# A two-block transformer kernel on one Trainium2 core: tokens loaded feature-major in place of sixteen transposes, token-major rows loaded behind weight blob 2

## The chip, the core and the metric

One core of a Trainium2 chip. Five engines run side by side, each with an instruction stream of its own, tied together by semaphores: TensorE (PE, matmuls out of SBUF into PSUM), VectorE (DVE), ScalarE (ACT), GpSimd (POOL) and SyncE (SP), which issues DMAs. ACT issues some DMAs too. A DMA moves data between HBM and SBUF and raises its semaphore by 16 when it has landed. The metric is device microseconds for one execution.

## The reference

A token block x of 256 tokens by 1024 features (float32) goes through two transformer layers of different make. What matters here is the very beginning, the first layer's norm and its input projection:

```python
def rmsnorm(x, gain):
    xf = x.astype(jnp.float32)
    y = xf * lax.rsqrt(jnp.mean(xf * xf, axis=-1, keepdims=True) + NORM_EPS)
    return (y * gain.astype(jnp.float32)).astype(x.dtype)
...
    proj = jnp.einsum('bsd,dn->bsn', xn, w_in)
    q_a, k_a, v_a, q_r, k_r, v_r, g_r, gate_a, gate_r = jnp.split(proj, IN_OFFSETS, axis=-1)
...
    h = x
    for l in range(DEPTH):
        h = h + mixer_block(rmsnorm(h, norm_mix_gain[l]), w_in[l], b_gates[l], attn_sinks[l],
                            ret_gn_gain[l], w_att_up[l], w_ret_up[l], w_out[l], att_rope, ret_rope)
        h = h + squared_relu_mlp(rmsnorm(h, norm_mlp_gain[l]), w_ff1[l], w_ff2[l])
```

Behind it come attention with a window, retention, gates, a feed-forward layer, and then a whole second block with its own weights. The change touches nothing of these.

## The kernel before, in words

**Weights.** All weight matrices are one stream of blobs of 128 partitions by 2048 float32 (1 MB each), numbered n = 0, 1, 2, ... SP loads blob n into `raw` (four buffers in the first layer). Every matmul is made of three products of float32r numbers: a number is split in a high part and a rest. ACT writes `whi` = high part of `raw` (function `hi`, L701), DVE writes `wlo` = `raw` - `whi` (function `lo`, L1621), and PE computes high x high (L477), high x rest (the line that the trace shows as L478 or L479) and rest x high for each piece (helper `product`, called by `multiply_tokens`). SP loads blob n + 4 into the buffer of blob n once `lo(n)` is done.

**Tokens.** `h` [128, 2, 1024] holds the 256 tokens token-major: partition = token in a tile of 128, two tiles t. A matmul that contracts over features needs them feature-major: `xT_h` and `xT_l` (high part and rest of gain times x), eight chunks k of 128 features by 256 tokens. The factor 1/rms of each token is applied after the matmul, by `stat`, when results leave PSUM.

**The start.** Before the change PE turns `h` into feature-major form: 16 transposes of 128x128 (`pieces(0, ...)`, L1185), two to a piece, eight pieces, listed in `XT_ORDER[0]` and placed in PSUM banks by `XT_PLACE[0]`. ACT scales each piece by the gain and writes `xT_h` (L717); DVE writes `xT_l` from the same PSUM piece (`to_pieces`, L1655). Blobs 0 and 1 are loaded and split in the parts of the table `FIRST` (blob, first chunk, last chunk + 1): five parts. PE multiplies part by part with pieces of transposes between them. Blob 0 feeds chunks 0 to 3 and blob 1 chunks 4 to 7; each chunk is 6 matmuls of 512 columns, so the two are 48. Blob 2 is 48 matmuls of 256 columns over all eight chunks, and every later blob of the projection is 24 matmuls of 512 columns. Before the first piece PE runs matmuls on zeros (`keep_warm`, L1207).

**The norm.** ACT squares the lower half of `h` with a running sum (L707), DVE the upper half (`square_upper`, L1630), DVE adds the shares (L1641) and POOL makes 1/rms (L1124). ACT waits for that before it takes the first results out of PSUM (L779).

**What sets the order.** Each engine runs its program in the order in which it is written. On DVE the two `square_upper` stand in front of `lo(2)`; on ACT `hi(2)` stands in front of the two squares and `hi(3)` behind them. On SP the DMAs are issued one after another on one queue; ACT issues the load of the first quarter of `h`. The load of `h` is in four quarters of the features, on the semaphores `x_in[0..3]`.

Of the kernel before, what the change touches and what calls it, by code (L numbers as in the profile page):

```python
# [80 lines left out]
for _name, _width in (("sinks", A_HEADS * 2), ("sinks_2", S_HEADS), ("lambdas", 4 * DH)):  # L81
# [3 lines left out]

XT_ORDER = (((0, 0), (1, 0), (0, 2), (1, 2), (0, 4), (1, 4), (0, 6), (1, 6)),
# [3 lines left out]
XT_PLACE = ((2, 3, 4, 5, 6, 7, 2, 3), (2, 3, 4, 6, 2, 3, 5, 7), (0, 1, 4, 6, 0, 1, 5, 7), (2, 3, 4, 5, 6, 7, 4, 5))  # L90

FIRST = ((0, 0, 1), (0, 1, 2), (0, 2, 4), (1, 0, 2), (1, 2, 4))

# [59 lines left out]

def build(nc, w, x, meta, consts, turns, rows, grow, out):

    with ExitStack() as ctx:
        def sem(name):
            return ctx.enter_context(nc.semaphore(name))
# [478 lines left out]
        def _(sp):  # L637
# [7 lines left out]

            def load_tokens(q):

                sp.dma_start(h[:, :, q * TOK:(q + 1) * TOK], x[:, :, q * TOK:(q + 1) * TOK]).then_inc(x_in[q], 16)

# [6 lines left out]
            load_first(1)  # L656
            load_tokens(1)
            load_first(2)
            load_tokens(2)
            load_first(3)  # L660
            load_tokens(3)
            load_first(4)
            load(2, w[2], None)
            load(3, w[3], None)
            sp.dma_start(cst[:, EARLY:NCONST], consts[:, EARLY:NCONST]).then_inc(const_in, 16)
# [27 lines left out]
        def _(act):  # L693
# [17 lines left out]
            def to_pieces(r, gain, pieces):  # L711

                for i in pieces:
                    act.wait_ge(xt_ps, 8 * r + i + 1)
                    t, k0 = XT_ORDER[r][i]
                    for k in range(2):
                        act.activation((xT_h if r < 2 else x2_h)[:, k0 + k, t * P:(t + 1) * P], piece(r, i, k), ACT.Copy,  # L717
                                       scale=cl(gain, k0 + k)).then_inc(xt_hi, 1)
# [30 lines left out]

            act.dma_start(h[:, :, 0:TOK], x[:, :, 0:TOK]).then_inc(x_in[0], 16)  # L750

            act.wait_ge(init_ok, 1)
            act.activation(lam[:], kaT[:, 0, 0:4], ACT.Copy)
            def first_part(i):
# [4 lines left out]
                               ACT.Copy).then_inc(split_hi if end == 4 else first_hi, 1)  # L759

            act.wait_ge(early_in, 16)
            to_pieces(0, "norm_mix", (0, 1))
            first_part(1)
            first_part(2)
            to_pieces(0, "norm_mix", (2, 3))
            to_pieces(0, "norm_mix", (4, 5))
            first_part(3)
            first_part(4)
            to_pieces(0, "norm_mix", (6, 7))
            hi(2)  # L770
            square(0)
            square(1)
# [392 lines left out]
        def _(pe):  # L1165
            ident = c("ident")

            def pieces(r, which):

                for i in which:  # L1170
                    t, k0 = XT_ORDER[r][i]
                    if r == 0:
                        pe.wait_ge(x_in[k0 // 2], 16)
                        if i >= 6:
                            pe.wait_ge(xt_lo, 2 * (i - 5))
                    elif r < 3:
                        pe.wait_ge(h_ok, 4 * (r - 1) + 2 * (k0 // 4) + t + 1)
# [44 lines left out]
            pe.wait_ge(early_in, 16)  # L1222
            pieces(0, (0, 1))
            keep_warm(2, 1, warm)
            for i, (n, k, end) in enumerate(FIRST):
                pe.wait_ge(split_lo if end == 4 else first_lo, first_made(i))
                multiply_tokens(pe, n, 4 * n, 4, BANK, 0, n == 0, n == 1, xT_h, xT_l, 0, ks=range(k, end))
                if i < 3:
                    pieces(0, (2 * i + 2, 2 * i + 3))
            for n in range(2, MIX1):  # L1230
# [377 lines left out]
        def _(dve):  # L1608
# [239 lines left out]
            def first_part(i):  # L1848
# [3 lines left out]
                if i:  # L1852
                    dve.wait_ge(split_hi if end == 4 else first_hi, first_made(i) - (end < 4))
                dve.tensor_tensor(wlo[n][:, a:b], raw[n][:, a:b], whi[n][:, a:b],  # L1854
                                  ALU.subtract).then_inc(split_lo if end == 4 else first_lo, 1)

            dve.wait_ge(early_in, 16)
            dve.wait_ge(first_in[0], 16)
            link(dve, "dve", dve.tensor_copy(whi[0][:, 0:BANK], raw[0][:, 0:BANK]))
            first_part(0)  # L1860
            to_pieces(0, "norm_mix", (0, 1))
            first_part(1)
            first_part(2)
            to_pieces(0, "norm_mix", (2, 3))
            to_pieces(0, "norm_mix", (4, 5))
            first_part(3)
            first_part(4)
            to_pieces(0, "norm_mix", (6, 7))
            dve.wait_ge(x_in[2], 16)
            dve.wait_ge(x_in[3], 16)  # L1870
            square_upper(0)
# [183 lines left out]
            dve.wait_ge(row_in, 32)  # L2055
            dve.wait_ge(xt_ps, 24)
            dve.wait_ge(rstd_ok, norms[0])
# [381 lines left out]
```

## Time and profile before

| what | value |
|---|---|
| median of 3 runs | 885.03 us (882.45, 885.03, 885.08) |
| the profiled execution's own time | 883.24 us |
| its span, first to last instruction | 881.6 us |
| PE busy | 871.6 us (99%) |
| DVE busy | 622.4 us (71%) |
| ACT busy | 459.4 us (52%) |
| DMA | 154.64 MB, mean 175 GB/s |

The span is the time from the first instruction to the last; 1.6 us lie around it. PE is busy nearly throughout, with its clock granted in full on the page, and DVE and ACT prepare the blobs ahead of it. The bandwidth is 345 and 401 GB/s in the first two slices of 22 us and about 200 GB/s after them.

### The profile page before, as it was taken

To read this page: it belongs to the slowest core of one execution; us is meant where nothing else is said; L and a number is where in the kernel's file an instruction comes from. 1 tells how busy PE (TensorE), PEld (TensorE's weight loads), DVE (VectorE), ACT (ScalarE), POOL (GpSimd) and SP (SyncE) were. 2 spreads that over 40 slices of the span, in tenths; PEclk is the share of its full clock that TensorE was granted. 3 is DMA by queue.
4 is the path that set the end of the run, shared out by engine and by line. 5 is a ranking of instruction groups with operands and counts; after the bars stand their busy time and mean duration, and the time that the engine had idled before them with its cause. 6 is when DMAs were issued, how large, how long until landed. Compare 5 with 4: busy or idle time off the path is not lost.

```text
span 881.6 us, 12940 instructions
## 1 busy us (share of the span) xinstructions
PE 871.6 (99%) x4790; PEld 730.9 (83%) x4790; DVE 622.4 (71%) x994; ACT 459.4 (52%) x742; POOL 45.2 (5%) x81
## 2 busy tenths in 40 slices
PE   8999999999999999999999999999999999999997
PEld 5887788888888888889998777777888888888886
DVE  6867677665876666668855778887766876666665
ACT  6546534334744444444546666677643654444443
POOL 0100010000200000002000000122300100000000
PEclk9999999999999999999999999999999999999999
DMA  9954344553565555343662223423274365555441
GB/s 345 401 206 180 128 159 143 191 191 143 205 237 193 188 192 190 145 167 122 215 254 98 101 114 115 148 97 144 96 262 174 109 233 184 187 195 187 186 143 48
DMA packets 24733, 154.64 MB, mean 175 GB/s; under 512 B 2912, under 2 KB 4192, under 8 KB 7280
## 3 DMA queue, kind: packets, MB, share of 16 engines
q1 hardware_dynamic: 22224, 146.61, 46.1%
q10 hardware_dynamic: 2464, 7.42, 2.3%
q8 instruction: 29, 0.48, 0.2%
q14 instruction: 16, 0.13, 0.0%
HBM read 151.58 MB, written 1.05 MB: 173 GB/s over the span
## 4 chain that ended last, share of the span: by engine, by line
PE 94%; DVE 3%; ACT 1%; DMA 1%; issue 0%; DVEq 0%; SPq 0%; ACTq 0%
PE ps L477 21%; PE ps L479 20%; PE ps L478 20%; PE ps L597 15%; PE ps L599 8%; PE ps L1510 2%; PE ps L1436 1%; PE ps L1460 1%; PE ps L1185 1%; DMA raw<-weights 1%; DVE sc L1820 1%; PE ps L614 1%; PE ps L1455 1%; DVE wlo L1621 0%; ACT sc L960 0%; PE ps L1450 0%
## 5 line engine op out<-in xcount | busy, mean ns | idle before, releaser
L1621 DVE TENSOR_TENSOR wlo<-raw,whi 128x2048 fp32r<-128x2048 f32 x134 | 306.7, 2290 | 148.5 <-ACT whi L701 148.1
L701 ACT ACTIVATE whi<-raw 128x2048 fp32r<-128x2048 f32 x134 | 256.4, 1916 | 182.5 <-PE ps L479 114.5
L477 PE MATMUL ps<-whi,xT 128*128 128x512 f32 (+1 forms) x224 | 88.0, 393 | 0.5 <-DVE xT L1655 0.5
L479 PE MATMUL ps<-whi,xT 128*128 128x512 f32 (+1 forms) x224 | 85.8, 383 | 0.0
L478 PE MATMUL ps<-wlo,xT 128*128 128x512 f32 (+1 forms) x224 | 85.6, 382 | 0.0
L597 PE MATMUL ps<-x_all,whi 128*128 128x512 f32 x336 | 84.0, 392 | 0.0
L597 PEld LDWEIGHTS ps<-x_all,whi 128*128 128x128 f32 x336 | 61.0, 189 | 11.3
L477 PE MATMUL ps<-whi,x_all 128*128 128x512 f32 x160 | 65.8, 411 | 0.4 <-ACT qbT L967 0.2
L597 PE MATMUL ps<-xT,whi 128*128 128x512 f32 x256 | 64.5, 392 | 0.0
L479 PE MATMUL ps<-whi,x_all 128*128 128x512 f32 x160 | 62.6, 391 | 0.0
L478 PE MATMUL ps<-wlo,x_all 128*128 128x512 f32 x160 | 62.4, 390 | 0.0
L597 PEld LDWEIGHTS ps<-xT,whi 128*128 128x128 f32 x256 | 46.3, 189 | 8.5
L477 PE MATMUL ps<-whi,fT_h 128*128 128x512 f32 x128 | 50.3, 393 | 0.0
L477 PEld LDWEIGHTS ps<-whi,xT 128*128 128x128 f32 x224 | 42.1, 188 | 9.7 <-DVE wlo L1854 1.3
L478 PE MATMUL ps<-wlo,fT_h 128*128 128x512 f32 x128 | 49.9, 390 | 0.0
L479 PE MATMUL ps<-whi,fT_l 128*128 128x512 f32 x128 | 49.8, 389 | 0.0
L479 PEld LDWEIGHTS ps<-whi,xT 128*128 128x128 f32 x224 | 42.1, 188 | 8.5
L599 PEld LDWEIGHTS ps<-x_all,wlo 128*128 128x128 f32 x336 | 45.8, 190 | 3.3
L478 PEld LDWEIGHTS ps<-wlo,xT 128*128 128x128 f32 x224 | 42.2, 188 | 7.5
L960 ACT ACTIVATE sc<-sc,usoft 128x272 f32<-128x272 f32 x64 | 32.7, 512 | 28.1 <-DVE usoft L1829 14.1
L599 PE MATMUL ps<-x_all,wlo 128*128 128x256 f32 x336 | 46.8, 282 | 0.0
L477 PE MATMUL ps<-x_all,whi 128*128 128x272 f32 x160 | 46.7, 292 | 0.0
(323 smaller groups left out, 1628.5 us busy)
## 6 DMA issues: line engine op xcount, KB each, us to landing
raw<-weights SPq DMA_DIRECT2D x134, 1024.0 KB, 4.8
raw<-weights SPq DMA_DIRECT2D x3, 512.0 KB, 7.3
cst<-consts SPq DMA_DIRECT2D x1, 1499.0 KB, 14.0
kswap<-kraw SPq DMA_DIRECT2D x20, 68.0 KB, 2.0
gate_a<-gain_rows ACTq DMA_DIRECT2D x2, 512.0 KB, 7.1
gate_r<-gain_rows ACTq DMA_DIRECT2D x2, 512.0 KB, 5.2
gate_s<-gain_rows ACTq DMA_DIRECT2D x2, 512.0 KB, 7.8
gate_d<-gain_rows ACTq DMA_DIRECT2D x2, 512.0 KB, 4.3
```

The lines of the kernel that those rows point to most:

```text
L477: pe.matmul(o, lh, rh, start=first, stop=False)
L478: pe.matmul(o, lh, rl, start=False, stop=False)
L479: return pe.matmul(o, ll, rh, start=False, stop=last)
L597: pe.matmul(ps[:, bank0 + j, :], vh[:, k, j * P:(j + 1) * P], x[:, :, k, :], start=k == 0, stop=False)
L599: m = pe.matmul(ps[:, bank0 + j, 0:TOK], vl[:, k, j * P:(j + 1) * P], x[:, 0, k, :], start=False, stop=k == KC - 1)
L614: pe.matmul(o, vh[:, k, j * P:(j + 1) * P], x[:, :, k, t * P:(t + 1) * P], start=k == 0, stop=False)
L701: act.activation(whi[s][:], raw[s][:], ACT.Copy).then_inc(split_hi, 1)
L960: ins = act.activation(scores(U, u), scores(U, u), ACT.Exp, bias=st[:, 2, u:u + 1], accum_out=st[:, 4, u:u + 1])
L1185: m = pe.transpose(piece(r, i, k), h[:, t, (k0 + k) * P:(k0 + k + 1) * P], ident)
L1436: pe.transpose(ps[:, 6, (2 * u + kt) * P:(2 * u + kt + 1) * P], scores_of_tile(U, u, kt), ident)
L1510: m = pe.matmul(ps[:, 4 + u, 0:KEYS], qT[half, cc, t * P:(t + 1) * P], kT, start=True, stop=True)
L1621: dve.tensor_tensor(wlo[s][:], raw[s][:], whi[s][:], ALU.subtract).then_inc(split_lo, 1)
```

## The change

The host passes x a second time, as `x_features`: 128 partitions by 8 chunks by 256 tokens, feature-major. SP and ACT load it in four quarters into a new tile `xF` (which lies where `gr` comes later), on `x_in[0..3]`. ACT and DVE make `xT_h` and `xT_l` straight from `xF`, a chunk of 128x256 at a time (`features_hi`, `features_lo`), where they read 128x128 pieces of PSUM before. PE does no transposes for this round; the other rounds of transposes stay. The token-major `h` is still needed by the norm and the residual: SP loads it whole, 1 MB in one DMA on a new semaphore `tok_in`, behind blob 2 and ahead of blob 3. ACT waits for `tok_in` between `hi(2)` and the squares; DVE waits for it in front of `square_upper`, which still stands ahead of `lo(2)`. Blob 0 is loaded and split in four parts where it was three.

```diff
-XT_ORDER = (((0, 0), (1, 0), (0, 2), (1, 2), (0, 4), (1, 4), (0, 6), (1, 6)),
+XT_ORDER = ((),
...
-FIRST = ((0, 0, 1), (0, 1, 2), (0, 2, 4), (1, 0, 2), (1, 2, 4))
+FIRST = ((0, 0, 1), (0, 1, 2), (0, 2, 3), (0, 3, 4), (1, 0, 2), (1, 2, 4))
...
+        xF = at("xF", [P, KC, TOK], F32, gr_at)
...
-            def load_tokens(q):
-
-                sp.dma_start(h[:, :, q * TOK:(q + 1) * TOK], x[:, :, q * TOK:(q + 1) * TOK]).then_inc(x_in[q], 16)
+            def load_features(q):
+
+                sp.dma_start(xF[:, 2 * q:2 * q + 2, :], x_features[:, 2 * q:2 * q + 2, :]).then_inc(x_in[q], 16)
...
             load_first(0)
             load_first(1)
-            load_tokens(1)
+            load_features(1)
             load_first(2)
-            load_tokens(2)
             load_first(3)
-            load_tokens(3)
+            load_features(2)
             load_first(4)
+            load_features(3)
+            load_first(5)
             load(2, w[2], None)
+            sp.dma_start(h[:], x).then_inc(tok_in, 16)
             load(3, w[3], None)
...
-            act.dma_start(h[:, :, 0:TOK], x[:, :, 0:TOK]).then_inc(x_in[0], 16)
+            act.dma_start(xF[:, 0:2, :], x_features[:, 0:2, :]).then_inc(x_in[0], 16)
...
+            def features_hi(q):
+
+                act.wait_ge(x_in[q], 16)
+                for k in (2 * q, 2 * q + 1):
+                    act.activation(xT_h[:, k, :], xF[:, k, :], ACT.Copy, scale=cl("norm_mix", k)).then_inc(xt_hi, 2)
+
             act.wait_ge(early_in, 16)
-            to_pieces(0, "norm_mix", (0, 1))
+            features_hi(0)
             first_part(1)
+            features_hi(1)
             first_part(2)
-            to_pieces(0, "norm_mix", (2, 3))
-            to_pieces(0, "norm_mix", (4, 5))
             first_part(3)
+            features_hi(2)
             first_part(4)
-            to_pieces(0, "norm_mix", (6, 7))
+            features_hi(3)
+            first_part(5)
             hi(2)
+            act.wait_ge(tok_in, 16)
             square(0)
             square(1)
...
             pe.wait_ge(early_in, 16)
-            pieces(0, (0, 1))
             keep_warm(2, 1, warm)
             for i, (n, k, end) in enumerate(FIRST):
                 pe.wait_ge(split_lo if end == 4 else first_lo, first_made(i))
-                multiply_tokens(pe, n, 4 * n, 4, BANK, 0, n == 0, n == 1, xT_h, xT_l, 0, ks=range(k, end))
-                if i < 3:
-                    pieces(0, (2 * i + 2, 2 * i + 3))
+                pe.wait_ge(xt_lo, 2 * (4 * n + end))
+                multiply_tokens(pe, n, 4 * n, 4, BANK, 0, n == 0, n == 1, xT_h, xT_l, ks=range(k, end))
...
+            def features_lo(*ks):
+
+                for k in ks:
+                    dve.wait_ge(xt_hi, 2 * (k + 1))
+                    dve.scalar_tensor_tensor(out=xT_l[:, k, :], in0=xF[:, k, :], scalar=cl("norm_mix", k),
+                                             in1=xT_h[:, k, :], op0=ALU.mult, op1=ALU.subtract).then_inc(xt_lo, 2)
+
             dve.wait_ge(early_in, 16)
+            features_lo(0)
             dve.wait_ge(first_in[0], 16)
             link(dve, "dve", dve.tensor_copy(whi[0][:, 0:BANK], raw[0][:, 0:BANK]))
             first_part(0)
-            to_pieces(0, "norm_mix", (0, 1))
+            features_lo(1)
             first_part(1)
+            features_lo(2, 3)
             first_part(2)
-            to_pieces(0, "norm_mix", (2, 3))
-            to_pieces(0, "norm_mix", (4, 5))
             first_part(3)
+            features_lo(4, 5)
             first_part(4)
-            to_pieces(0, "norm_mix", (6, 7))
-            dve.wait_ge(x_in[2], 16)
-            dve.wait_ge(x_in[3], 16)
+            features_lo(6, 7)
+            first_part(5)
+            dve.wait_ge(tok_in, 16)
             square_upper(0)
             square_upper(1)
             lo(2)
```

How the instructions stand in a row. SP, the queue of DMA issues from its second instruction on, before. `raw_49`, `raw_52`, `raw_55` and `raw_58` are the buffers of blobs 0, 1, 2 and 3:

```order
L644 DMA cst<-consts 128x250
L653 DMA raw_49<-weights 128x512 x2
L648 DMA h<-x_tiles 128x2x256
L653 DMA raw_49<-weights 128x1024
L648 DMA h<-x_tiles 128x2x256
L653 DMA raw_52<-weights 128x1024
L648 DMA h<-x_tiles 128x2x256
L653 DMA raw_52<-weights 128x1024
L642 DMA raw_55<-weights 128x2048
L642 DMA raw_58<-weights 128x2048
```

SP, the same place after:

```order
L646 DMA cst<-consts 128x250
L655 DMA raw_49<-weights 128x512 x2
L650 DMA xF<-x_features 128x512
L655 DMA raw_49<-weights 128x512 x2
L650 DMA xF<-x_features 128x512
L655 DMA raw_52<-weights 128x1024
L650 DMA xF<-x_features 128x512
L655 DMA raw_52<-weights 128x1024
L644 DMA raw_55<-weights 128x2048
L667 DMA h<-x_tiles 128x2048
L644 DMA raw_58<-weights 128x2048
```

The quarters of `xF` stand where quarters of `h` stood, and the whole `h` takes the place that blob 3 had.

DVE from its third instruction on, the splits of blobs 0 to 2, before. `wlo_51`, `wlo_54` and `wlo_57` are the rests of blobs 0, 1 and 2; the two ISA lines with `xn` are `square_upper`:

```order
L1859 CAST whi_50<-raw_49 128x512
L1854 TENSOR_TENSOR wlo_51<-raw_49,whi_50 128x512
L1655 SCALAR_TENSOR_TENSOR xT<-ps,cst,xT 128x128 x4
L1854 TENSOR_TENSOR wlo_51<-raw_49,whi_50 128x512
L1854 TENSOR_TENSOR wlo_51<-raw_49,whi_50 128x1024
L1655 SCALAR_TENSOR_TENSOR xT<-ps,cst,xT 128x128 x8
L1854 TENSOR_TENSOR wlo_54<-raw_52,whi_53 128x1024 x2
L1655 SCALAR_TENSOR_TENSOR xT<-ps,cst,xT 128x128 x4
L1630 ISA xn,stat<-h 128x512
...
L1621 TENSOR_TENSOR wlo_57<-raw_55,whi_56 128x2048
```

DVE, the same place after:

```order
L1867 SCALAR_TENSOR_TENSOR xT<-xF,cst,xT 128x256
L1873 CAST whi_50<-raw_49 128x512
L1860 TENSOR_TENSOR wlo_51<-raw_49,whi_50 128x512
L1867 SCALAR_TENSOR_TENSOR xT<-xF,cst,xT 128x256
L1860 TENSOR_TENSOR wlo_51<-raw_49,whi_50 128x512
L1867 SCALAR_TENSOR_TENSOR xT<-xF,cst,xT 128x256 x2
L1860 TENSOR_TENSOR wlo_51<-raw_49,whi_50 128x512 x2
L1867 SCALAR_TENSOR_TENSOR xT<-xF,cst,xT 128x256 x2
L1860 TENSOR_TENSOR wlo_54<-raw_52,whi_53 128x1024
...
L1636 ISA xn,stat<-h 128x512
...
L1627 TENSOR_TENSOR wlo_57<-raw_55,whi_56 128x2048
```

The first rest of x stands ahead of blob 0's first part; one chunk of it, where four pieces were, stands between the first two parts; the squares of `h` still stand ahead of the split of blob 2.

## Rows read from the trace of the kernel before

**Rows 1.** PE's waits over the whole span; columns: engine, tile, line, releaser, us, times, longest.

```profile
PE ps L1207 <- DVE kaT L1847: 1.4, 1, 1.4
PE ps L1185 <- DMA h<-x_tiles: 1.2, 1, 1.2
PE ps L477 <- DVE xT L1655: 0.5, 1, 0.5
```

**Rows 2.** Timeline, 0 to 10 us: start, us, engine, line, operation, tiles, count [idle before].

```profile
5.96 0.63 PE L1185 MATMUL ps<-cst,h 128*128 128x128 f32 x4 [1.21 <-DMA h<-x_tiles]
6.47 1.14 ACT L717 ACTIVATE xT<-ps,cst 128x128 fp32r<-128x128 f32 x4 [3.56 <-PE ps L1185]
6.76 0.43 DVE L1859 CAST whi<-raw 128x512 fp32r<-128x512 f32 x1 [5.37 <-DMA raw<-weights]
7.22 0.69 DVE L1854 TENSOR_TENSOR wlo<-raw,whi 128x512 fp32r<-128x512 f32 x1
7.83 1.12 DVE L1655 SCALAR_TENSOR_TENSOR xT<-ps,cst,xT 128x128 fp32r<-128x128 f32 x4
8.84 0.47 PE L477 MATMUL ps<-whi,xT 128*128 128x512 f32 x1 [0.53 <-DVE xT L1655]
```

**Rows 3.** Timeline, PE: behind the last transposes, first of blob 2, first of blob 3.

```profile
15.95 0.50 PE L477 MATMUL ps<-whi,xT 128*128 128x512 f32 x1
...
21.54 0.39 PE L477 MATMUL ps<-whi,xT 128*128 128x256 f32 x1
...
27.38 0.40 PE L477 MATMUL ps<-whi,xT 128*128 128x512 f32 x1
```

**Rows 4.** All groups of instructions by form: line, forms, count, busy us, mean ns.

```profile
L1934 DVE SCALAR_TENSOR_TENSOR retT_l<-ps,cst,retT_h 128x256 fp32r<-128x256 f32 x8 | 3.5, 478 | 5.5 <-ACT retT_h L838 5.5
L838 ACT ACTIVATE retT_h<-ps,cst 128x256 fp32r<-128x256 f32 x8 | 3.3, 466 | 5.9 <-PE ps L1331 5.9
```

**Rows 5.** Timeline, ACT and DVE, 16 to 23 us: splits of blobs 2 and 3, squares.

```profile
16.97 1.93 ACT L701 ACTIVATE whi<-raw 128x2048 fp32r<-128x2048 f32 x1
...
17.98 0.68 DVE L1630 CUSTOM_DVE_ANT_0 xn<-h 128x512 f32<-128x512 f32 x1
...
19.20 2.29 DVE L1621 TENSOR_TENSOR wlo<-raw,whi 128x2048 fp32r<-128x2048 f32 x1
```

**Rows 6.** DMA issues and landings: tiles, queue, count, KB, us from issue to landing.

```profile
h<-x_tiles ACTq DMA_DIRECT2D x1, 256.0 KB, 5.1
...
raw<-weights SPq DMA_DIRECT2D x1, 1024.0 KB, 9.6
...
raw<-weights SPq DMA_DIRECT2D x1, 1024.0 KB, 11.6
...
raw<-weights SPq DMA_DIRECT2D x1, 1024.0 KB, 12.9
```

**Rows 7.** Timeline, SP's queue, the issues of blobs 2, 3 and, from 11.94, 4 and later.

```profile
6.24 0.91 SPq L642 DMA_DIRECT2D raw<-weights  x2
```

**Rows 8.** Busy time of three stretches: us, engines, PEclk, DMA share, GB/s (last).

```profile
3.00:5.50 2.50, 1.75 (x3) 0.34 (x1) 0.00 (x0) 0.00 (x0) 0.00 (x0) 1.00 0.74 168
5.50:8.00 2.50, 2.04 (x8) 1.07 (x8) 1.20 (x3) 1.53 (x5) 0.00 (x0) 1.00 1.03 383
8.00:18.00 10.00, 9.47 (x46) 7.44 (x46) 8.28 (x21) 7.41 (x17) 0.00 (x0) 1.00 1.04 421
```

**Rows 9.** Timeline, PE's weight loads for the matmuls on zeros, one to each matmul.

```profile
3.32 0.34 PEld L1207 LDWEIGHTS ps<-kaT 128*128 128x128 f32 x1 [0.52 <-issue]
...
7.29 0.19 PEld L1207 LDWEIGHTS ps<-kaT 128*128 128x128 f32 x1 [0.24 <-issue]
```

**Rows 10.** Timeline, 24 to 35 us: splits of blob 4 and PE's first matmul on it.

```profile
25.91 1.92 ACT L701 ACTIVATE whi<-raw 128x2048 fp32r<-128x2048 f32 x1
...
28.15 2.29 DVE L1621 TENSOR_TENSOR wlo<-raw,whi 128x2048 fp32r<-128x2048 f32 x1
...
33.87 0.48 PE L477 MATMUL ps<-whi,xT 128*128 128x512 f32 x1
```

More of the change, by code:

```diff
@@ L89 @@
             ((0, 0), (0, 2), (0, 4), (0, 6), (1, 0), (1, 2), (1, 4), (1, 6)))
-XT_PLACE = ((2, 3, 4, 5, 6, 7, 2, 3), (2, 3, 4, 6, 2, 3, 5, 7), (0, 1, 4, 6, 0, 1, 5, 7), (2, 3, 4, 5, 6, 7, 4, 5))
-FIRST = ((0, 0, 1), (0, 1, 2), (0, 2, 4), (1, 0, 2), (1, 2, 4))
+XT_PLACE = ((), (2, 3, 4, 6, 2, 3, 5, 7), (0, 1, 4, 6, 0, 1, 5, 7), (2, 3, 4, 5, 6, 7, 4, 5))
+FIRST = ((0, 0, 1), (0, 1, 2), (0, 2, 3), (0, 3, 4), (1, 0, 2), (1, 2, 4))
 def first_made(i):
@@ L151, in fills, with build @@
     return (N1 - 1) // 4 + 1 + (n - N1) // 3
-def build(nc, w, x, meta, consts, turns, rows, grow, out):
+def build(nc, w, x, x_features, meta, consts, turns, rows, grow, out):
     with ExitStack() as ctx:
@@ L323, in build @@
         x_in = [sem(f"x_in{i}") for i in range(4)]
+        tok_in = sem("tok_in")
         early_in = sem("early_in")
@@ L713, in to_pieces @@
                 for i in pieces:
-                    act.wait_ge(xt_ps, 8 * r + i + 1)
+                    act.wait_ge(xt_ps, 8 * (r - 1) + i + 1)
                     t, k0 = XT_ORDER[r][i]
@@ L1171, in pieces @@
                     t, k0 = XT_ORDER[r][i]
[L1172 to L1176, printed above, removed]
+                    if r < 3:
                         pe.wait_ge(h_ok, 4 * (r - 1) + 2 * (k0 // 4) + t + 1)
@@ L2055, in _ @@
             dve.wait_ge(row_in, 32)
-            dve.wait_ge(xt_ps, 24)
+            dve.wait_ge(xt_ps, 16)
             dve.wait_ge(rstd_ok, norms[0])
@@ L2407 @@
     x = i["x"][0].reshape(NT, P, D).transpose(1, 0, 2)
+    x_features = i["x"][0].T.reshape(KC, P, TOK).transpose(1, 0, 2)
     consts = constants()
@@ L2425 @@
         "x_tiles": x,
+        "x_features": x_features,
         "meta": i["meta_tokens_2"],
```

## The prediction, written before the changed kernel was run

> **What bounds the kernel now.** I read the waits of PE first [rows 1]. Over 881.6 us PE has three waits of 0.5 us or more, all in the first 9 us; what the view has beside them is 0.4 and 0.2. Everything after 8.84 us is one unbroken run of matmuls, so a microsecond that PE starts earlier, or is kept waiting once, should move the end by one microsecond. Then I read the timeline of the start [rows 2]. The chain to the first real matmul is: quarter 0 of `h` lands (5.96), PE transposes it, ACT makes the high parts (6.47), DVE meanwhile splits the first part of blob 0 (6.76 to 7.91) and only then makes the rests (7.83), and PE begins at 8.84. Last come the reads ahead of blob 2 [rows 3, 5]: PE starts blob 2 at 21.54 without a pause, and DVE ends the split of blob 2 at 19.20 + 2.29 = 21.49. The two meet within 0.05 us. That is the row on which my forecast hangs: PE cannot gain anything at this point unless `lo(2)` is earlier too.
>
> **Part 1: the transposes go.** Between 15.95 and 21.54 PE does 24 matmuls in 5.59 us, 0.233 us each [rows 3]. All 48 of blobs 0 and 1 are 11.18 us. From 8.84 to 21.54 they took 12.70, so the three groups of transposes between them cost 1.52 us in all. This goes away. The fourth group runs ahead of the first matmul and leaves the chain with it.
>
> **Part 2: the first matmul.** Quarter 0 now feeds ACT directly. It was issued at about 0.74 and landed 5.1 us later, 5.84 [rows 6]. No row has an activation of 128x256 from SBUF; from PSUM it takes 466 ns, and the matching DVE operation 478 ns [rows 4]. I take these, with 0.3 to 0.6 as bounds: the high part of chunk 0 at 6.35, its rest at 6.85. The first part of blob 0 was there at 6.76 [rows 2]; cast and rest take 0.43 + 0.69, so with handovers of about 0.03 each PE starts at 8.05. That is 0.8 us earlier (bounds 0.5 and 1.0). The Trainium skill, "VectorE: DVE Perf Modes", section "The TRN2 errata — SBUF-src ops pay a fixed extra latency per instruction", gives SBUF sources a smaller fixed cost than PSUM on VectorE (58 cycles against 120) and a larger one on ScalarE (224 against 172). An estimate by its figures puts the start 0.1 us earlier than mine and leaves the end of the forecast as it is. No run here shows it yet.
>
> **Part 3: supply of the eight chunks.** DVE's work on x shrinks from 16 operations to 8, blob 0 in four parts adds one. With landings as before, walking DVE's order in steps of 0.40 for a rest and 0.69 or 1.2 for a part gives: chunk 1 ready 9.1 (PE wants it 9.5), chunk 2 10.7 (10.9), chunk 3 11.3 (12.3), chunks 4 and 5 about 13.9 (13.7), chunks 6 and 7 about 15.9 (16.5). At most 0.3 us of stall. So PE would be through with blob 1 at 8.05 + 11.18 + about 0.2 = 19.4, some 2.1 us before 21.54. This is the whole prize of the change, and the trace of before has no other place for more.
>
> **Part 4: blob 2, where it is lost.** DVE waits for `tok_in` before the squares, and `lo(2)` is behind them. ACT has `hi(2)` ahead of its own wait, so that is not in the way. When does `h` land? Bytes ahead of and including it on the queue: constants 0.13 MB, blobs 0 and 1 2.10, features 1.05, blob 2 1.05, `h` 1.05: 5.37 MB. Before, the same sum up to and including blob 3 was 0.13 + 2.10 + 1.05 (tokens) + 1.05 + 1.05: 5.37 MB. `h` takes the place that blob 3 had. Blob 2 was issued at 6.24 and blob 3 about 0.48 later, at 6.72 [rows 7]; they landed 9.6 and 11.6 us after that [rows 6], at 15.8 and 18.3. The 2.5 us between them for 1.05 MB are 420 GB/s, and the ten microseconds up to 18.00 run at 421 GB/s with a DMA share of 1.04 [rows 8], so the DMA engines are full and nothing hides there. The quarters now have runs of 2 KB where they had 1 KB, which can only help; from 3.00 to 5.50 the rate is 168 GB/s at a share of 0.74, and from 5.50 it is 383 [rows 8]. If the low rate came from short runs, those 2.5 us could shrink by up to 1.4; if from starting up, by nothing, since DMA engines were partly idle then. I take 0.1: `h` lands at 18.2.
> From the start of the squares to the end of `lo(2)` DVE took 21.49 - 17.98 = 3.51 us [rows 5]. So `lo(2)` ends at 18.2 + 0.05 + 3.51 = 21.76 and PE starts blob 2 at about 21.8, where it was 21.54. PE waits some 2.4 us at this point, a wait that is new. The sum: -0.8 (start), -1.5 (transposes), +0.2 (chunk stalls), +2.4 (wait for blob 2) = **+0.3 us**. All of what is gained in parts 1 and 2 is given back in one wait. Bounds: -1.1 if the DMA start shrinks by all of 1.4, +0.6 if `h` is late by 0.3.
>
> **Part 5: behind blob 2.** The queue now carries 1.05 MB more ahead of everything later, 2.5 us at 421 GB/s. Blob 3 lands near 20.7; ACT and DVE have its rest at about 25, PE wants it at 27.6 (21.8 + 27.38 - 21.54). Blob 4, issued at 11.94, landed 12.9 later [rows 6], 24.8; now 27.3. Its high part began at 25.91 and begins at 27.3, its rest began at 28.15 and begins at about 29.2, ready 31.5 [rows 10]; PE wants it at 33.87 + 0.3. That leaves 2.6 us. The cover is this lead of DVE over PE; gone, each microsecond costs one. ACT waits behind `tok_in` with `hi(3)`, which waits for its own later load anyway. The split of `h` into one DMA, the changed counts of semaphores and the place of `xF` cost nothing: no engine is late at them.
>
> **The rivals.**
> *A, part of the gain stays (2 in 10).* The slow start of the DMAs was due to 1 KB runs, so `h` and blob 2 come up to 1.4 us earlier. `lo(2)` then ends near 20.4 and blob 2 starts near 20.5: up to -1.1. A little more would need DVE not to wait for `h` before `lo(2)`: blob 2 landed at 15.8, `hi(2)` takes 1.93 and `lo(2)` 2.29 [rows 5], so 20.1 and -1.4 would be the limit of an order with `lo(2)` first. The transfer rate above speaks against a large part of it: the engines were not full between 3.00 and 5.50.
> *B, slower: the new wait costs clock (1 in 10).* Matmuls on zeros ran one in 0.34 + 0.52 = 0.86 us at 3.32 and in 0.19 + 0.24 = 0.43 us at 7.29 [rows 9]: 1.2 and 2.4 GHz. The slow work went from 1.4 [rows 1] to 5.96 - 1.21 = 4.75 [rows 2], some 3.3 us, and behind the idle 1.21 us the engine was fast. No gap of 2.4 us stands in this trace once PE is fast. If such a gap takes the clock down and it needs 3.3 to 4.5 us of work to come back, that work takes twice its time: 1.7 to 2.2 us more, +2.0 to +2.5 in all. The 0.5 us ahead of 8.84 did not do it; the granted clock of the whole stretch up to 18.00 is 1.00 [rows 8]. For 2.4 us I have no row, so the case keeps a chance.
> *C, other (under 1 in 10).* Blob 4 or 5 comes more than 2.6 us later than I have it and PE waits a second time (+1 to +2), or DVE's order stalls PE in blob 0 by more than 0.3, which the wait at blob 2 would swallow.
>
> **How the numbers follow.** Forecast 65%, A 18%, B 10%, C 7%. Against the profiled execution: span 881.6 + 0.3 = 881.9, time 883.24 + 0.3 = 883.5. The median shown is 885.03, which is 1.8 above that execution, and the lowest run is 882.45; the spread of the four times, 2.6 us, is larger than any term of mine. On the median the sum is 885.3, on the middle of the four times (884.1) it is 884.4. I take 884.6. The range takes in A (884.1 - 1.1, less what the spread adds) and most of B: 882.2 to 886.8. A measurement of this kernel can tell about 0.3%, 2.65 us. The largest gain that any case holds is 1.1, so faster by that much needs luck with the spread: 5%. Slower needs B or C in full plus some spread: 6%. The rest, 89%, is no change.
>
> **What would show it.** Right: no PE idle time for transposes, first matmul near 8.05, one wait of PE near 19.4 to 21.8 released by `wlo` of blob 2, DVE idle from about 16 to 18.2 for the DMA of `h`, and PE unbroken after. Part 2 is wrong if the first matmul is not within 0.3 us of 8.05; part 3 if PE waits more than 0.5 us inside blobs 0 and 1; part 4 if `h` lands before 17.5 or DVE is not idle ahead of the squares; part 5 if PE waits at blob 3, 4 or 5. If the matmuls behind the wait have twice their spacing, B holds.

## The result, and the profile after

| | before | changed |
|---|---|---|
| median | 883.62 us (882.45 to 885.08, 12 runs) | 886.07 us (884.80 to 887.08, 12 runs) |
| profiled execution: time, span | 883.24, 881.6 | 887.08, 885.0 |
| first matmul on blob 0 | 8.84 us | 7.42 us |
| first matmul on blob 2 | 21.54 us | 23.59 us |

The ratio of changed to before is 1.0022, 95% interval 1.0014 to 1.0030. The changed kernel is some 2 us slower. That is below the 0.3% that I had named as what can be told, but twelve runs tell it from nothing, and I had forecast no change. One run of E9 below took 1447.29 us at a mean granted clock of 0.558 and stands outside every median and ratio here.

The first view is what PE waited for in the changed kernel, over the whole span (columns as in [rows 1]):

```profile
PE ps L479 <- DVE wlo L1627: 2.4, 1, 2.4
PE ps L479 <- DVE wlo L1860: 1.7, 2, 1.4
PE ps L1215 <- DVE kaT L1853: 1.4, 1, 1.4
PE ps L616 <- DVE x_all L1661: 0.4, 1, 0.4
```

L1627 is `lo`, L1860 the split of a part of blobs 0 and 1; in the changed kernel L479 is the product high x high that was L477. The wait for transposes is gone, and so is the one for `xT` in [rows 1]. Two new ones are there: 2.4 us for the rest of blob 2, as forecast, and 1.7 us inside blobs 0 and 1, where I had at most 0.3.

The timeline of the changed kernel, its main steps, in order of time (columns as in [rows 2]):

```profile
4.93 0.91 ACT L769 ACTIVATE xT<-xF,cst 128x256 fp32r<-128x256 f32 x2 [2.26 <-DMA xF<-x_features]
5.58 0.48 DVE L1867 SCALAR_TENSOR_TENSOR xT<-xF,cst,xT 128x256 fp32r<-128x256 f32 x1 [4.19 <-ACT xT L769]
...
7.42 0.84 PE L479 MATMUL ps<-whi,xT 128*128 128x512 f32 x1
...
11.02 0.63 ACT L762 ACTIVATE whi<-raw 128x512 fp32r<-128x512 f32 x1 [2.21 <-DMA raw<-weights]
...
12.43 0.50 PE L479 MATMUL ps<-whi,xT 128*128 128x512 f32 x1 [0.29 <-DVE wlo L1860]
...
15.46 0.50 PE L479 MATMUL ps<-whi,xT 128*128 128x512 f32 x1 [1.38 <-DVE wlo L1860]
...
17.53 1.92 ACT L705 ACTIVATE whi<-raw 128x2048 fp32r<-128x2048 f32 x1 [1.43 <-DMA raw<-weights]
...
20.02 0.69 DVE L1636 CUSTOM_DVE_ANT_0 xn<-h 128x512 f32<-128x512 f32 x1 [2.67 <-DMA h<-x_tiles]
...
21.25 2.29 DVE L1627 TENSOR_TENSOR wlo<-raw,whi 128x2048 fp32r<-128x2048 f32 x1
...
23.59 0.38 PE L479 MATMUL ps<-whi,xT 128*128 128x256 f32 x1 [2.40 <-DVE wlo L1627]
...
36.39 1.03 PE L1222 MATMUL ps<-cst,tok 128*128 128x128 f32 x8
```

The last line is the first transposes behind blob 3. In the kernel before they stand here:

```profile
32.86 1.03 PE L1214 MATMUL ps<-cst,tok 128*128 128x128 f32 x8
```

These answer [rows 2], [rows 3] and [rows 5]. Features are there at 4.93, a microsecond earlier than the quarter of `h` was. Then ACT waits 2.21 us at 11.02 for the fourth part of blob 0, and 1.43 at 17.53 for blob 2. DVE has been idle 2.67 us when `h` lands at 20.02; I had 18.2. From there to PE's first matmul on blob 2 the chain is what was forecast: 3.57 us.

Busy time by stretch of the changed kernel (columns as in [rows 8]; PEclk is third from the end):

```profile
6.00:8.00 2.00, 2.00 (x4) 0.74 (x3) 1.97 (x5) 1.26 (x3) 0.00 (x0) 1.00 1.07 339
8.00:10.00 2.00, 2.00 (x11) 1.62 (x10) 1.53 (x4) 0.81 (x2) 0.00 (x0) 1.00 0.94 245
10.00:12.00 2.00, 2.00 (x10) 1.45 (x8) 0.31 (x1) 0.74 (x2) 0.00 (x0) 1.00 1.04 412
24.00:26.00 2.00, 2.00 (x14) 2.00 (x14) 1.55 (x1) 1.49 (x3) 0.83 (x2) 0.65 1.03 427
26.00:28.00 2.00, 2.00 (x11) 2.00 (x11) 1.90 (x8) 0.19 (x1) 0.00 (x0) 0.50 1.02 426
```

Two things stand here that the sum of the forecast did not have. From 8 to 10 us the DMAs move 245 GB/s with engines that are 94% busy, where the kernel before moved 410 in the same two microseconds. And after the wait for blob 2 the granted clock is 0.50: 1.2 GHz instead of 2.4. Rival B happened.

**Where 3.4 us come from.** From the start of blob 0 to that of blob 2 the kernel before needs 12.70 us, the changed one 23.59 - 7.42 = 16.17. By starts of matmuls: first matmul earlier -1.42; transposes between the matmuls gone -1.52; the first matmuls still slow (7.42 took 0.84, though the granted clock of that stretch reads 1.00) about +0.5; stalls inside blobs 0 and 1 +2.0; wait at blob 2 +2.5. Sum +2.05. From the first matmul on blob 2 to the transposes behind blob 3 it takes 36.39 - 23.59 = 12.80 us, where it was 32.86 - 21.54 = 11.32: +1.48 for half clock. Together 3.5, of 3.4 in the spans. It can be told more shortly: `h` landed 1.8 us later than forecast (20.02 against 18.2), and the chain behind it sets the start of blob 2; so the earlier first matmul and the stalls inside blobs 0 and 1 change only how long PE waits there. Forecast 0.3, late landing 1.8 and half clock 1.5 make 3.6, of 3.4 in the spans. Around the span there is a little more as well: time minus span is 1.58 to 1.71 in every run of the kernel before and 1.78 to 2.11 in the changed one (E1 and E16 included).

### The profile page after: what moved, and what is told of

Read it like the earlier page. It is cut to its first block, busy times and chain, and to the rows that moved or that the text cites. A ratio compares the mean times of both kernels' runs of the same rounds, so it can differ in the third digit from the quotient of the medians.

```text
span 885.0 us, 12903 instructions
## 1 busy us (share of the span) xinstructions
PE 872.8 (99%) x4774; PEld 731.2 (83%) x4774; DVE 621.5 (70%) x987; ACT 459.4 (52%) x735; POOL 43.1 (5%) x81
## 3 DMA queue, kind: packets, MB, share of 16 engines
q10 hardware_dynamic: 2336, 7.42, 2.5%
## 4 chain that ended last, share of the span: by engine, by line
PE 93%; DVE 3%; DMA 1%; SPq 1%; ACT 1%; issue 0%; DVEq 0%; ACTq 0%
PE ps L479 20%; PE ps L481 19%; PE ps L480 19%; PE ps L599 15%; PE ps L601 8%; PE ps L1516 2%; DMA h<-x_tiles 1%; PE ps L1442 1%; PE ps L1466 1%; DVE wlo L1627 1%; PE ps L1193 1%; DVE sc L1826 1%; PE ps L616 1%; PE ps L1461 0%; ACT sc L972 0%
## 5 line engine op out<-in xcount | busy, mean ns | idle before, releaser
L1627 DVE TENSOR_TENSOR wlo<-raw,whi 128x2048 fp32r<-128x2048 f32 x134 | 306.6, 2290 | 151.5 <-ACT whi L705 151.2
L479 PE MATMUL ps<-whi,xT 128*128 128x512 f32 (+1 forms) x224 | 89.0, 397 | 4.1 <-DVE wlo L1627 2.4
L599 PEld LDWEIGHTS ps<-x_all,whi 128*128 128x128 f32 x336 | 61.0, 189 | 11.3
L479 PE MATMUL ps<-whi,x_all 128*128 128x512 f32 x160 | 65.8, 411 | 0.4 <-ACT qsT L979 0.2
L479 PEld LDWEIGHTS ps<-whi,xT 128*128 128x128 f32 x224 | 43.0, 192 | 13.8 <-DVE wlo L1860 3.0
L479 PE MATMUL ps<-whi,fT_h 128*128 128x512 f32 x128 | 50.3, 393 | 0.0
L479 PE MATMUL ps<-x_all,whi 128*128 128x272 f32 x160 | 46.7, 292 | 0.0
```

Source lines behind the costliest of these rows:

```text
L479: pe.matmul(o, lh, rh, start=first, stop=False)
L599: pe.matmul(ps[:, bank0 + j, :], vh[:, k, j * P:(j + 1) * P], x[:, :, k, :], start=k == 0, stop=False)
L1627: dve.tensor_tensor(wlo[s][:], raw[s][:], whi[s][:], ALU.subtract).then_inc(split_lo, 1)
```

## Experiments

All kernels below come from one of the two kernels by the edit shown. Ratios are to the kernel before, with 95% interval. "Lands" is the time of the waiting instruction behind the DMA.

**E1: the same kernel again**, and once more as E16.

> The changed kernel once more, unedited. Theory (the late landing of h belongs to the kernel): first matmul of blob 0 near 7.4 us, rate of the DMAs from 6.5 to 9.5 us again well under 383 GB/s, h lands near 20.0, blob 2 starts near 23.6 and the matmuls behind it run at half clock for some 3.5 us; ratio to before 1.002 to 1.004. Rival (the one profiled execution was an unlucky one): h lands near 18.2, blob 2 starts near 21.8, no half clock.

> The changed kernel, a third profile. Theory: features and four parts make the DMAs slow between 6 and 10 us (rates 245 to 340 GB/s from 8 to 10 us), h lands between 18.6 and 20.0, blob 2 starts between 22.2 and 23.6, PE waits 2.4 us for it; whether half clock follows differs from execution to execution (it did in one of two). Rival: the second profile (h at 18.6) was the rule and 20.0 the exception, or the other way round.

E1: 884.70 us (10 runs), ratio 1.0016 (1.0004 to 1.0027). E1's timeline:

```profile
18.63 0.69 DVE L1636 CUSTOM_DVE_ANT_0 xn<-h 128x512 f32<-128x512 f32 x1 [2.65 <-DMA h<-x_tiles]
...
22.20 0.39 PE L479 MATMUL ps<-whi,xT 128*128 128x256 f32 x1 [2.37 <-DVE wlo L1627]
```

and E16's:

```profile
19.49 0.69 DVE L1636 CUSTOM_DVE_ANT_0 xn<-h 128x512 f32<-128x512 f32 x1 [2.65 <-DMA h<-x_tiles]
...
23.06 0.39 PE L479 MATMUL ps<-whi,xT 128*128 128x256 f32 x1 [2.37 <-DVE wlo L1627]
```

The landing of `h` moves between 18.6 and 20.0 from execution to execution, with rates of 335, 288 and 245 GB/s from 8 to 10 us; the wait at blob 2 is 2.4 us each time. The spans are 882.2, 883.0 and 885.0. E1 and E16 keep the full clock behind the wait, the first profile does not. So the slow DMAs belong to the kernel, and the half clock to some of its executions. E1's profile is close to the forecast (span 882.2 against 881.9), the first one is not, and the median of E1's ten runs is 1.4 us under that of the first twelve: how much is lost differs from one set of runs of the same kernel to the next.

**E2: DVE splits blob 2 before it waits for h.**

```diff
-            dve.wait_ge(tok_in, 16)
-            square_upper(0)
-            square_upper(1)
             lo(2)
+            dve.wait_ge(tok_in, 16)
+            square_upper(0)
+            square_upper(1)
```

> DVE splits blob 2 before it waits for h and squares it. Theory (the wait for h in front of the split is what costs): blob 2 lands at 17.5, high part 1.93, rest 2.29, so blob 2 starts near 21.8 instead of 23.6; PE's wait there shrinks from 2.4 to about 0.6 us, no half clock follows; span 1.8 + 1.5 = 3.3 us shorter than the changed kernel, near 881.7, ratio to before 0.999 to 1.001. Rival (the lead of DVE is used up anyway, so the later squares and 1/rms hold up the first results out of PSUM): a wait of PE at blob 3 takes the place, gain under 1 us.

883.83 us, ratio 1.0007 (0.9996 to 1.0018), span 881.8; E1, measured beside it, has 884.70. Its waits of PE:

```profile
PE ps L479 <- DVE wlo L1860: 2.1, 2, 1.8
...
PE ps L479 <- DVE wlo L1627: 0.6, 1, 0.6
PE ps L1274 <- DVE ka_tok L1706: 0.5, 1, 0.5
```

The wait at blob 2 shrinks from 2.4 to 0.6 us, blob 2 starts at 21.19, and the clock stays, though a gap of 1.8 us stands inside blobs 0 and 1. `square_upper` in front of `lo(2)`, on a later load, was the wait. A new small one appears behind blob 3: blob 4 lands at 28.33 here (its split began at 25.91 before, [rows 10]), ACT has the split of blob 4 ahead of its copy of `ka_tok`, and PE waits 0.5 us for that.

```profile
28.33 1.92 ACT L705 ACTIVATE whi<-raw 128x2048 fp32r<-128x2048 f32 x1 [3.31 <-DMA raw<-weights]
```

My part 5 had looked for the landing of blob 4 only against PE's use of blob 4, not against what is queued behind it on ACT.

**E3: the gap is filled, the wait kept.**

```diff
+                if n == 2:
+                    keep_warm(2, 7, warm)
                 if n < MIX1 - 2:
                     pe.wait_ge(split_lo, n + 1)
```

> Two matmuls of 512 columns on zeros into an unused PSUM bank between blobs 1 and 2, 1.7 us of the 2.4 us that PE waits there; no wait is taken away. Theory (the idle time takes the clock down): blob 2 starts as late as in the changed kernel, near 23.6, but runs at 0.12 us a matmul throughout; span 1.5 us shorter, near 883.5. Rival (the half clock has nothing to do with the gap): half clock as before, span unchanged or longer.

884.57 us, ratio 1.0011 (1.0000 to 1.0022), span 882.5, full clock. `h` landed at 19.0 in its profile and blob 2 started late, at 22.59:

```profile
22.59 0.38 PE L479 MATMUL ps<-whi,xT 128*128 128x256 f32 x1 [0.66 <-DVE wlo L1629]
```

Since one profile can keep its clock by luck, the count over runs says more. A run's mean granted clock of 0.997 or less stands in 18 of 42 runs of the kernels with an idle gap of 2.4 us or more at blob 2 (the changed kernel, E1, E4, E7) and in none of 10 of this one. That count, with the profiles, speaks for the gap as what lets the clock fall; it does not fall each time. It also stands in none of 10 runs of E8, whose gap is 1.7 us, but in 2 of 10 of E2, with 0.6 us at blob 2 and 1.8 further ahead. In E1, E4 and E7 the runs with the lowered clock are 0.9 to 1.3 us longer than the others; in the first twelve they are not (886.11 against 886.00). And the time of E3 hardly moved: 884.57 beside E1's 884.70, where 1.5 us less in some executions had been expected. So what the half clock costs over many runs is not well shown.

**E4: each quarter of the features contiguous in HBM.**

```diff
-                sp.dma_start(xF[:, 2 * q:2 * q + 2, :], x_features[:, 2 * q:2 * q + 2, :]).then_inc(x_in[q], 16)
+                sp.dma_start(xF[:, 2 * q:2 * q + 2, :], x_features[q]).then_inc(x_in[q], 16)
...
-    x_features = i["x"][0].T.reshape(KC, P, TOK).transpose(1, 0, 2)
+    x_features = i["x"][0].T.reshape(4, 2, P, TOK).transpose(0, 2, 1, 3)
```

> The host lays each quarter of the feature-major tokens out as one contiguous 256 KB, where it was 128 runs of 2 KB, 8 KB apart. Tile, order and bytes are the same. Theory a (runs of 2 KB at a pitch of 8 KB are what slows the DMAs between 6.5 and 9.5 us): the rate there goes to 380 to 420 GB/s and h lands near 18.5, span 1.5 to 3 us shorter than the changed kernel. Theory b (the pattern in HBM does not matter; what slows is something else, such as the number of DMAs or the stall of the issuing queue at 6.12 us): h lands within 0.3 us of where it does now, span unchanged.

885.71 us, ratio 1.0019 (1.0007 to 1.0031), span 883.6. Its stretches:

```profile
8.00:10.00 2.00, 2.00 (x10) 1.46 (x8) 1.27 (x3) 1.69 (x4) 0.00 (x0) 1.00 1.04 411
24.00:26.00 2.00, 2.00 (x11) 2.00 (x11) 1.93 (x6) 0.67 (x2) 0.00 (x0) 0.50 1.01 419
```

The rate goes to 411 GB/s and `h` lands at 18.50, as theory a said; the stalls in blobs 0 and 1 fall to 0.8 us. The time gains nothing: theory a had the span 1.5 to 3 us shorter, and the median is 1.0 us above that of E1, measured beside it. PE waits 2.39 us at blob 2 all the same, this profile has half clock behind it, and 6 of the 10 runs have a mean clock of 0.997 or less. It is one profile, but its 411 stands outside the 245 to 340 of the six profiles with the strided layout and four parts (the changed kernel, E1, E2, E3, E7, E16); its landing, 18.50, is just ahead of E1's 18.63.

**E8: blob 0 in three parts again.**

```diff
-FIRST = ((0, 0, 1), (0, 1, 2), (0, 2, 3), (0, 3, 4), (1, 0, 2), (1, 2, 4))
+FIRST = ((0, 0, 1), (0, 1, 2), (0, 2, 4), (1, 0, 2), (1, 2, 4))
```

(and the calls that go with it).

> The changed kernel with blob 0 in three parts again, as before (undoes one part of the change). Theory (short runs at a pitch of 8 KB slow the DMAs from 6.5 to 9.5 us, and the fourth part made two more of them): the rate from 8 to 10 us rises from 245 to 335 to near 400 GB/s, h lands at 18.3 to 18.6, span 0.3 to 1 us shorter. Rival (only the features' layout matters): rate and landing as in the changed kernel, 18.6 to 20.0; the part of chunks 2 and 3 comes later and PE waits 0.5 to 1 us more inside blob 0, which the wait at blob 2 hides.

883.46 us, ratio 0.9991 (0.9979 to 1.0004), span 881.6. E7 (below), which has four parts and was measured beside it, has 884.76; nine of E8's ten runs lie below E7's lowest. Stretch and timeline:

```profile
8.00:10.00 2.00, 2.00 (x9) 1.28 (x7) 1.16 (x3) 1.70 (x4) 0.00 (x0) 1.00 1.00 381
```

```profile
17.91 0.69 DVE L1634 CUSTOM_DVE_ANT_0 xn<-h 128x512 f32<-128x512 f32 x1 [2.65 <-DMA h<-x_tiles]
...
21.48 0.39 PE L479 MATMUL ps<-whi,xT 128*128 128x256 f32 x1 [1.66 <-DVE wlo L1625]
```

With three parts `h` lands at 17.9, and in the two later kernels with three parts (E10, E11) at 18.6 and 18.0: mean 18.2, which is the number of my part 4. With four parts, the six profiles give 18.6 to 20.0, mean 19.3. So the number was right for a queue with the old parts, and the fourth part of blob 0 costs some 1.1 us of landing in the mean; single profiles overlap (18.6 stands in both). The rate says less: from 8 to 10 us the three profiles with three parts have 381, 377 and 344 GB/s, and E7 with four has 340. PE also still waits 1.3 us inside blob 0 here. Nothing in the sum had a price for the fourth part but "adds one operation".

**E9, E12, E15: four parts alone, in the kernel before.**

> The kernel before with blob 0 in four parts, the one part of the change alone; tokens, transposes and the load of h stay as before. Theory (the two loads of 2 KB runs in place of one of 4 KB runs slow the DMAs): the rate from 8 to 10 us falls from 404-410 to 300-350 GB/s, blob 2 lands 0.5 to 1 us later than 15.8, blob 2 starts 0.3 to 1 us later than 21.0-21.5, ratio 1.0003 to 1.001. Rival (it takes the feature loads beside it): rate and landing as before, ratio within 0.0005 of 1.

> The kernel before with blob 0 in four parts once more, profiled again: nearly all of its times lie in the upper group (884.2 to 885.9), so this profile should show one such execution. Theory (the upper group is half clock behind the idle time ahead of the first transposes): span near 883.3, the transposes or the matmuls of blobs 0 and 1 run at half clock for 2 to 4.5 us, and blob 2 starts about 2 us later than 20.8. Rival (DMA): full clock, the loads of blobs 0 to 2 land 1 to 2 us later than 15.9, and PE waits for a part.

> The kernel before with blob 0 in four parts, one more profile; 10 of its 11 undisturbed times were of the upper group, so this has the best chance to show one. Same two expectations: half clock for 3 to 4 us in or behind the start, or late loads at full clock.

E9: 885.07 us (11 runs), ratio 1.0013 (1.0003 to 1.0023). From 8 to 10 us the three profiles have 394, 372 and 368 GB/s, where the kernel before has 398 to 410 in four; from 10 to 12 they have 390, 374 and 361, where it has 397 to 417. The fall is there, but smaller than the expected one: beside tokens in runs of 1 KB the fourth part costs less than beside features. Blob 2 starts at 20.81, 21.29 and 20.81, no later than before. Nine of E9's eleven runs lie in the upper group of times that the next experiments are about, but its profiled executions (spans 881.1, 881.7, 881.1) do not show why; that stays open. (The expectation of E15 says ten of eleven; it is nine.)

**E5, E13, E14, E6: the two groups of times of the kernel before.** Its times lie in two groups, most of them from 882.5 to 883.5 or from 884.4 to 886. E6 is the kernel before with one more matmul on zeros:

```diff
             pe.wait_ge(early_in, 16)
+            keep_warm(1, 1, warm, TOK + P)
             pieces(0, (0, 1))
```

> The kernel before once more, unedited, profiled again. Its times fall in two groups, 882.5 to 883.3 and 884.6 to 885.7. Theory (the upper group is half clock in the start, since PE is idle for 1.2 us before the first transposes): a profile with a span near 881 has its first transposes 0.63 us long and the matmul on zeros behind them 0.43 us apart; one with a span near 883.3 has slow ones up to about 10 us, or a stretch of half clock behind a gap. Rival (the upper group comes from DMAs or from far behind in the kernel): the start and the clock are the same in both.

> The kernel before with one more matmul of 384 columns on zeros ahead of the first transposes, which fills the idle 1.2 us between 4.75 and 5.96. Theory (that idle time is what makes the upper group): nearly all times in the lower group, median 882.8, ratio 0.998 to 0.999. Rival: the shares of the two groups stay near 6 to 4.

> The kernel before, one more profile, to see an execution of the upper group of its times (884.2 and more, near half of them). Theory (half clock in or behind the start): span 882.6 or more with a stretch of 3 to 4 us where matmuls on blobs 0 to 2 stand at twice their distance, blob 2 starting near 23 us or ending late. Rival (DMA): the same clock, blob 0's parts land 1 to 2 us later. A span near 881 says nothing on it.

> The same once more, with the same two expectations; an execution of the lower group (span 881.0 to 881.6) says nothing on the upper one.

E6: 883.19 us, all ten runs between 882.59 and 883.72, ratio 0.9992 (0.9980 to 1.0004). The runs of the kernel before beside it had 15 of 31 below 884.1, E5 (884.41 us) 3 of 10. So the upper group goes away when PE is kept busy ahead of the first transposes, as the theory said of the times. But the profiles of E5, E13 and E14 (spans 881.1, 881.4 and 881.5) all show the lower group with the full clock and on-time loads. No profile showed an execution of the upper group; that it is half clock is argued and not shown. The mean granted clocks do not settle it: over all runs of the kernel before that were measured beside E1 to E16, 12 of the 51 in the upper group have 0.997 or less and none of the 51 in the lower, so some of the upper ones did lose clock; but 30 have 0.999, and slow matmuls of the start do not show in this number.

**E7: both layouts of x in one input tensor.**

```diff
-        "x_tiles": x,
-        "x_features": x_features,
+        "x_tiles": np.stack([x.reshape(P, NT * D), x_features.reshape(P, NT * D)]),
```

> The changed kernel with the two layouts of x in one input tensor. Time minus span is 1.6 to 1.7 us for the kernel before and 1.8 to 2.1 for the changed one. Theory (it is the fourteenth tensor): the difference goes back to 1.65, 0.3 us. Rival (it is something else in the program's ending or start): it stays near 1.95. DMAs, h's landing and the gap stay as in the changed kernel.

884.76 us, ratio 1.0012 (0.9998 to 1.0026), span 882.9. Time minus span stays at 1.83 to 2.03 us, so the theory of the extra tensor fell. Four parts alone (E9) have 1.76 to 1.84, the changed kernel with three parts (E8) 1.84 to 2.05. What makes the 0.3 us around the span stays open.

**E10 and E11: a version that beats both.** E10 is E8 with the order of E2. E11 then moves the late constants:

```diff
             load(3, w[3], None)
+            load(4, w[4], 1)
             sp.dma_start(cst[:, EARLY:NCONST], consts[:, EARLY:NCONST]).then_inc(const_in, 16)
             sp.dma_start(row[:], rows.partition_broadcast(P)).then_inc(const_in, 16)
-            with sp.Fori(4, N1 - 4, 4) as i:
+            for n in range(5, 8):
+                load(n, w[n], n - 3)
+            with sp.Fori(8, N1 - 4, 4) as i:
```

> The changed kernel with both edits: blob 0 in three parts, and DVE splits blob 2 ahead of its wait for h. Theory: blob 2 lands at 15.4 to 15.9, so its rest is ready at 19.7 to 20.2, about when PE ends blob 1 (19.8); no wait there, blob 2 starts 1.3 to 1.8 us earlier than in the kernel before. Then blob 4, which lands 1 to 2 us later than before because h went ahead of it, holds up ACT's copy of ka_tok, and PE waits 1 to 2 us for it behind blob 3, so half or more of the gain goes there: span 880.5 to 881.3. Rival (blob 4 is early enough): span 879.8 to 880.2.

> The same with the late constants and rows (1.68 MB, first needed at about 39 us) issued behind blob 4 instead of ahead of it. Theory (blob 4's landing is what is late behind blob 3): blob 4 lands near 24 instead of 27, no wait of PE at ka_tok, span 879.6 to 880.2, median 0.997 to 0.9985 of the kernel before. Rival (ACT's and DVE's own order behind blob 3 is what holds ka_tok up): the wait stays, span as in the other one.

E10: 883.76 us, ratio 1.0000 (0.9991 to 1.0009), span 881.8, where 880.5 to 881.3 had been expected; the better order of DVE gained nothing over E8 by itself. Its profile fell to half clock early, behind a stall of 1.8 us in blob 0:

```profile
12.08 0.50 PE L479 MATMUL ps<-whi,xT 128*128 128x512 f32 x1 [1.78 <-DVE wlo L1858]
```

```profile
12.00:14.00 2.00, 1.92 (x7) 1.59 (x8) 2.00 (x5) 1.93 (x4) 0.00 (x0) 0.83 1.02 432
14.00:16.00 2.00, 2.00 (x6) 1.52 (x6) 1.97 (x4) 0.71 (x1) 0.00 (x0) 0.50 1.01 426
```

PE was then so late (blob 2 at 22.0) that the wait at `ka_tok` could not show; the rope of `ka_tok` ended at 33.3, and PE came to it at about 34. With blob 2 at 19.9 PE would have come to it near 32, an estimated wait of 1.2 us, as expected; this profile does not show it.

E11: 881.76 us (881.35 to 882.44, 12 runs), ratio 0.9974 (0.9965 to 0.9983), span 880.2:

```profile
19.87 0.39 PE L479 MATMUL ps<-whi,xT 128*128 128x256 f32 x1
```

```profile
31.20 1.03 PE L1223 MATMUL ps<-cst,tok 128*128 128x128 f32 x8
32.07 0.38 PE L1275 MATMUL ps<-cst,ka_tok 128*128 128x128 f32 x2
```

Blob 2 starts 1.67 us earlier than in the kernel before and the transposes behind blob 3 stand 1.66 us earlier than the first profile of that kernel has them (its other three start blob 2 at 20.99 to 21.43), without a wait. Between E10 and E11 only the late constants moved behind blob 4 (the loads of blobs 5 to 7 are written out for it), and that is 2 us in the median. With the order of DVE, the parts and the constants mended, the features as a host layout are worth 0.26%. The new orders were not tried on the kernel before, which has no wait there for them to take away.

## Why the prediction was wrong, point by point

- **Part 1, transposes: right.** PE does none between the parts. E11 starts blob 2 at 19.87: its first matmul at 7.12, 11.18 for the 48 matmuls, 1.1 of waits and some 0.5 for the slow first matmul.
- **Part 2, first matmul: the mechanism right, the size too small.** -1.42 us against -0.8 (the first matmul stands at 8.28 to 8.84 in four profiles before, at 6.99 to 7.42 in three of the changed kernel). The quarter of `xF` landed at 4.93 and blob 0's first part early enough for the cast at 5.99; I had held both at the landings of before. The activation of 128x256 from SBUF measured 499 ns and the DVE operation 480, inside my bounds. The Trainium skill, "VectorE: DVE Perf Modes", section "The TRN2 errata — SBUF-src ops pay a fixed extra latency per instruction", gives 224 cycles plus one per element at 1.2 GHz on ScalarE and 58 plus one per element at 0.96 GHz on VectorE; an estimate by these is 400 and 327 ns. Both measured longer. Against the same sizes from PSUM [rows 4], ScalarE took 33 ns more from SBUF, the sign that the page has, and VectorE 2 ns more, where the page has less.
- **Part 3, supply of the chunks: wrong.** At most 0.3 us of stall was forecast, and 1.7 came (0.9 in E1 and 1.8 in E16, without the wait ahead of the first matmul). The step that failed is "with landings as before": chunk 3 was ready at 12.4 where I had 11.3, chunks 4 and 5 at 15.4 where I had 13.9. PE also wanted chunk 3 some 0.3 us earlier than forecast. The fourth part is not all of it: with three, PE still waits 1.0 to 1.8 us there (E8, E10, E11), with contiguous quarters 0.8 (E4).
- **Part 4, the wait at blob 2: the mechanism right, its terms mis-sized.** This is the term that decides the time. PE waits 2.4 us there in every profile of the changed kernel. That this is the forecast to the tenth is luck: both ends of the wait are later, PE's end of blob 1 (21.2 in the first profile, where I had 19.4) and the start of blob 2. The mis-sized term is the landing of `h`, forecast at 18.2 because it "takes the place that blob 3 had" in a queue at 420 GB/s: it measured 20.02, 19.49 and 18.63, and blob 2 started at 23.59, 23.06 and 22.20 in place of 21.8. From 3.00 to 5.50 the rate did rise, from 168 to 278 GB/s; from 8 to 10 us it fell to 245 to 335. So runs of 2 KB in place of 1 KB "can only help" does not hold for the stretch as a whole. E8 undoes the fourth part and lands at 17.9; E2 takes most of the wait away.
- **Part 5, behind blob 2: right while PE is late, wrong otherwise.** No wait showed in the changed kernel. E2 shows that `ka_tok` behind blob 4's split is late next (0.5 us), at less than the 2.6 us that I had as cover, and E11 that it is on time once blob 4 goes ahead of the constants. The nearest cover in the kernel before was there, from the end of its rope at 31.81 to PE's use at 33.73, 1.9 us:

```profile
31.62 0.19 DVE L1700 TENSOR_TENSOR ka_tok<-ka_tok,scratch 128x32 f32<-128x32 f32 x1
33.73 0.38 PE L1268 MATMUL ps<-cst,ka_tok 128*128 128x128 f32 x2
```

- **Rival A: not so.** The quarters did come earlier, but the stretch behind them got slower, not faster.
- **Rival B: it happened**, in some executions: +1.48 us in the first profile, half clock from about 24.6 to 28. I had it at one in ten and +1.7 to +2.2. By the count above it is nearer to two in five. It is the second step that failed: the chance of B was too low.
- **Clear of noise or not.** I took the spread of the times for noise of 0.3%. It is two groups, and with ten or twelve runs beside some thirty of the other kernel about 0.1% can be told.

An estimate of the whole: the forecast had +0.3; the landing of `h` adds about +1.1 on average over it, half clock +0.6 (1.5 in two of five), and the time around the span +0.3: 2.3, of 2.45 between the medians. That it comes so close is partly luck. The terms are from profiles, which for the kernel before are all of its lower group, while its median of 883.62 lies between the groups; against the middle of the lower group, 882.9, the changed kernel's median is 3.2 us longer, and 0.9 stays unexplained.

## What to carry to other kernels

A wait for a load belongs behind all work that does not need the load, on each engine's stream; here the split of blob 2 stood behind a wait for tokens that only the norm wanted, and one moved line was worth 0.9 us in the median (E2 beside E1). When a load is cut in smaller parts or put ahead of others, price it by the rate of the whole queue and by everything behind it, late constants included: moving them (2.0 us from E10 to E11) was worth more than the three groups of transposes (1.5 us). And a saved microsecond on an engine at 99% is only saved if it isn't turned into a gap, because a gap can cost the clock on top.

## What the runs showed of the hardware that I had not expected

- The clock of TensorE fell from 2.4 to 1.2 GHz behind idle gaps of 2.4 us (the changed kernel, E4) and 1.8 us (E10), and did not behind gaps of 2.4 to 2.7 us in E1, E16 and E7 or of 1.8 in E2 and E16. In the changed kernel it stood at 0.50 from 24.6 to 28.0 us, and blobs 2 and 3 took 1.5 us longer, in E4 as well (12.82 us in place of 11.32).
- DMA engines read as 92 to 102% busy moved 245 to 340 GB/s from 8 to 10 us (six profiles), where the kernel before moved 398 to 410 at 104 to 106%. It came with loads of 2 KB runs at a pitch of 8 KB, features and parts of blob 0 in a row; contiguous quarters brought 411, three parts 344 to 381. Why is not shown.
- The issue of a DMA can itself take long: SP's issue of blob 2 took 2.01 us in the changed kernel, 1.73 in E16, 1.38 in E7, 1.36 in E3 and 0.60 in E1, where the issue ahead of it took 0.6. `h` landed at 20.02, 19.49, 19.35, 19.02 and 18.63 in them: later where the issue took longer. Which of the two causes the other, or whether a third thing causes both, is not shown.

```profile
6.12 2.01 SPq L644 DMA_DIRECT2D raw<-weights  x1
```
